# Second MLP up-projection: both halves of the activation in one 512-column pass, the convolution chain spread over later steps

## The reference

```python
def conv_ffn(h, w_up, conv_w, conv_b, w_down):
    S = h.shape[1]
    u = h @ w_up                                   # 2048 -> 2*5632
    up = jnp.pad(u, ((0, 0), (CONV_WIDTH - 1, 0), (0, 0)))
    y = conv_b
    for i in range(CONV_WIDTH):                    # 3 taps over the tokens
        y = y + up[:, i:i + S] * conv_w[i]
    a, g = jnp.split(y, 2, axis=-1)
    return (jax.nn.silu(g) * a) @ w_down           # 5632 -> 2048
# every layer:  x = x + g1 * mixer(modulate(rms_norm(x)));  x = x + g2 * conv_ffn(modulate(rms_norm(x)))
```

## Time and profile before

| | us |
|---|---|
| median of 3 runs | 2096.26 |
| lowest, highest | 2095.01, 2097.05 |
| profiled execution, first to last instruction | 2094.6 |
| PE busy in it | 2030.2 |
| DVE busy | 1631.6 |
| ACT busy | 1012.0 |

### The profile page before, as it was taken

One profiled execution on the slowest core, in us unless ns is written; L12 is line 12 of the kernel. 1 busy time (PEld: TensorE's weight loads), 2 busy tenths in 40 slices (PEclk: granted clock), 3 DMA queues, 4 the chain that ended last, 5 costly groups with the idle time before them and its releaser, 6 DMA issues.

```text
span 2094.6 us, 36723 instructions
## 1 busy us (share of the span) xinstructions
PE 2030.2 (97%) x13730; PEld 1876.4 (90%) x13730; DVE 1631.6 (78%) x2277; ACT 1012.0 (48%) x1347; POOL 308.1 (15%) x459
## 2 busy tenths in 40 slices
PE   3999999998999999999999999899999999999998
PEld 3888989888999889999899987799988999889986
DVE  5786898987899988898989977888765565556565
ACT  4323675545555444554445455554443454434453
POOL 3232342220111221121122100011000000000000
PEclk8999999999999999999999999999999999999999
DMA  9999899884889999888998874487655555565552
GB/s 360 355 356 329 299 336 331 298 308 173 303 313 317 333 349 338 297 308 310 363 326 322 314 268 140 141 298 279 239 190 188 185 185 184 182 200 165 197 181 101
DMA packets 235842, 558.28 MB, mean 267 GB/s; under 512 B 14024, under 2 KB 15032, under 8 KB 235192
## 3 DMA queue, kind: packets, MB, share of 16 engines
q1 hardware_dynamic: 180408, 355.03, 49.1%
q0 software_dynamic: 55296, 201.35, 26.7%
HBM read 554.23 MB, written 2.10 MB: 266 GB/s over the span
## 4 chain that ended last, share of the span: by engine, by line
PE 86%; DVE 6%; issue 3%; ACT 2%; DMA 2%; POOL 0%; DVEq 0%; ACTq 0%; POOLq 0%
PE ps L636 16%; PE ps L638 16%; PE ps L637 16%; PE ps L664 10%; PE ps L666 10%; PE ps L665 10%; PE ps L684 3%; DVE w_lo L1372 2%; DVE macc L1386 1%; PE ps L681 1%; PE ps L702 1%; DMA mraw<-in_w_mod 1%; ACT w_hi L1032 1%; ACT work L1032 1%; DMA early<-in_w_mod 1%
## 5 line engine op out<-in xcount | busy, mean ns | idle before, releaser
L1032 ACT ACTIVATE w_hi<-raw 128x1024 fp32r<-128x1024 f32 x640 | 666.1, 1056 | 769.3 <-PE ps L638 483.5
L1372 DVE TENSOR_TENSOR w_lo<-raw,w_hi 128x1024 fp32r<-128x1024 f32 x640 | 766.8, 1225 | 339.9 <-ACT w_hi L1032 339.3
L636 PE MATMUL ps<-h_hi,w_hi 128*128 128x256 f32 x3200 | 913.7, 286 | 1.4 <-DVE w_lo L1372 1.2
L638 PE MATMUL ps<-h_hi,w_lo 128*128 128x256 f32 x3200 | 906.7, 283 | 0.0
L637 PE MATMUL ps<-h_lo,w_hi 128*128 128x256 f32 x3200 | 906.7, 283 | 0.0
L636 PEld LDWEIGHTS ps<-h_hi,w_hi 128*128 128x128 f32 x3200 | 615.7, 192 | 4.9 <-issue 4.7
L637 PEld LDWEIGHTS ps<-h_lo,w_hi 128*128 128x128 f32 x3200 | 615.8, 192 | 2.1 <-issue 1.9
L638 PEld LDWEIGHTS ps<-h_hi,w_lo 128*128 128x128 f32 x3200 | 615.4, 192 | 0.0
L1386 DVE SCALAR_TENSOR_TENSOR macc<-mraw,cond,macc 128x512 f32<-128x512 f32 x620 | 427.8, 746 | 52.7 <-DMA mraw<-in_w_mod 44.4
L521 POOL DMA_DIRECT2D mraw<-in_w_mod x358 | 258.7, 723 | 1176.5 <-DVE macc L1386 868.4
L664 PE MATMUL ps<-w_hi,g_hi 128*128 128x512 f32 x832 | 326.1, 392 | 1.5 <-DVE w_lo L1372 1.5
(11 more groups left out here) (164 smaller groups left out, 1139.0 us busy)
## 6 DMA issues: line engine op xcount, KB each, us to landing
mraw<-in_w_mod POOLq DMA_DIRECT2D x358, 512.0 KB, 6.5
raw<-in_w_up SPq DMA_DIRECT2D x176, 1024.0 KB, 5.3
raw<-in_w_down SPq DMA_DIRECT2D x88, 1024.0 KB, 5.9
raw<-in_w_attn_in SPq DMA_DIRECT2D x48, 1024.0 KB, 8.7
raw<-in_w_attn_out SPq DMA_DIRECT2D x16, 1024.0 KB, 7.3
work<-in_w_mod POOLq DMA_DIRECT2D x12, 512.0 KB, 8.7
early<-in_w_mod POOLq DMA_DIRECT2D x8, 512.0 KB, 12.6
raw<-in_w_pool SPq DMA_DIRECT2D x4, 1024.0 KB, 5.4
```

The costliest lines, as they stand in the source:

```text
L636: mm(o, wh, ah, start=st, stop=False, skip_group_check=True)
L638: i = mm(o, wl, ah, start=False, stop=last_half and kk == 1, skip_group_check=True)
L1032: return nc.scalar.activation(o, i, f, **kw)
L1372: V.tensor_tensor(w_lo[:, s, :, :], raw[:, j % 4, h * 1024:(h + 1) * 1024].rearrange("p (k n) -> p k n", k=2), w_hi[:, s, :, :].bitcast(F3 ...
```

## The change

Layer 1's MLP becomes `mlp_second`, written out without hardware loops; layer 0's (`mlp_first`) stays as it was. In `mlp_second`:

- `h_hi` and `h_lo` become two halves of one tensor `h_pair`, and one matmul streams both (512 columns) against the same `w_hi`. Its result fills a whole bank: the first 256 columns hold high x high, the last 256 high x low. The third product (low x high, 256 columns) is added to the first 256.
- A half thus takes four banks: half 0 and half 1 of a pair have banks 0 to 3 and 4 to 7 or the reverse (`wide_bank`).
- ACT copies the last 256 columns of the four banks to `low` (SBUF), DVE adds the first 256 and frees the banks; the taps then read `low`.
- The taps are done a step later (`a` in step 4, `g` in step 0 of the next pair), silu and product in step 1, `g_hi` and `g_lo` in step 2; after the last pair of a block, in steps 0 to 2 of `down`.
- `gate_sum` comes before unit 3 of the next pair and writes bank 4; `gate_row` is in DVE's step 3; PE waits for it before half 1 (unit 4), which writes that bank.
- The last block's `down` takes its units in another order (`LAST_DOWN`).

```diff
-        h_hi = sb("h_hi", [P, KT, SEQ], F32R)
-        h_lo = sb("h_lo", [P, KT, SEQ], F32R)
+        h_pair = sb("h_pair", [P, KT, 2, SEQ], F32R)
+        h_hi, h_lo = h_pair[:, :, 0, :], h_pair[:, :, 1, :]
...
+        def wide_bank(block, half):
+            return (4 * (block % 2) + 4 * half) % 8
...
+        LAST_DOWN = [(0, 0), (0, 1), (1, 0), (1, 1), (0, 2), (1, 2),
+                     (2, 0), (2, 1), (2, 2), (3, 0), (3, 1), (3, 2)]
...
+            def unit_wide(q, j, k0, first, last, bank, h_need):
+                for half in range(2):
+                    pe.wait_ge(hlo_ready, h_need + k0 + 2 * half + 2)
+                    low_at, s0 = split_at(q, j)
+                    pe.wait_ge(lo_ready, low_at + half + 1)
+                    s = (s0 + half) % 4
+                    for kk in range(2):
+                        k = k0 + 2 * half + kk
+                        for t in range(4):
+                            wh, wl = (w[:, s, kk, t * P:(t + 1) * P] for w in (w_hi, w_lo))
+                            mm(ps[:, bank + t, :], wh, h_pair[:, k, :, :].rearrange("p a t -> p (a t)"),
+                               start=first and half == 0 and kk == 0, stop=False, skip_group_check=True)
+                            i = mm(ps[:, bank + t, 0:SEQ], wl, h_pair[:, k, 0, :], start=False,
+                                   stop=last and half == 1 and kk == 1, skip_group_check=True)
+                    i.then_inc(sub_used, 1)
...
+            def mlp_second():                      # PE
...
+                        for half in range(2):
+                            group_slot_free(g + 2 * i + half)
...
+                            if block == 0 and i and half:
+                                pe.wait_ge(mod_ready, 44 + i)
...
+                            for ks in range(4):
+                                if block == 0 and i and half == 0 and ks == 3:
+                                    group_slot_free(g + 2 * i + 1)
+                                    gate_sum(43 + i, i % 2)
+                                unit_wide(q + 2 * i + half, ks, 4 * ks, ks == 0, ks == 3,
+                                          wide_bank(block, half), KT * 3)
...
+                        for u in range(16):        # down, blocks 0 and 1
...
+                            pe.wait_ge(glo_ready, 2 * (11 + g0 + u % 4 + 1))
+                            unit_tok(q + u // 4, u % 4, 4 * (u % 4), u % 4 == 0, u % 4 == 3, g_hi, g_lo,
+                                     slot + u // 4 % 2)
...
+            def low_copy(used, bank, groups):      # ACT
+                act.wait_ge(sub_used, used)
+                if groups:
+                    act.wait_ge(taps_done, 2 * groups)
+                for b in range(2):
+                    A(low[:, 2 * b:2 * b + 2, :], ps[:, bank + 2 * b:bank + 2 * b + 2, SEQ:2 * SEQ],
+                      ACT.Copy).then_inc(low_out, 1)
...
+            def low_add(groups, bank):             # DVE
+                for b in range(2):
+                    dve.wait_ge(low_out, 2 * groups + b + 1)
+                    V.tensor_tensor(low[:, 2 * b:2 * b + 2, :], ps[:, bank + 2 * b:bank + 2 * b + 2, 0:SEQ],
+                                    low[:, 2 * b:2 * b + 2, :], ALU.add).then_inc((bank0_free, bank1_free)[b], 1)
...
+                    def pair_end(i, j):            # DVE
+                        if j == 0:
+                            earlier_taps(yg, 4 * p + FT, 8 * (11 + p) + 4, g + 2 * i + 1)
+                        elif j == 1:
+                            dve.wait_ge(taps_done, 4 * p + 2)
+                            gate_product(11 + p)
+                        elif j == 2:
+                            gated_lo(11 + p, i)
...
+                        for j in range(8):         # DVE, the steps of a pair
...
+                                piece(44 + i, at, (i + 1) % 2)
+                                piece(44 + i, at + 1, (i + 1) % 2)
+                            if not (p == 0 and j < 2):
+                                split(q + 2 * i, j + 2)
+                            if i and j < 3:
+                                pair_end(i - 1, j)
+                            if block == 0 and i and j == 3:
+                                gate_row(43 + i)
+                            if j == 4:
+                                earlier_taps(ya, 4 * p, 8 * (11 + p), g + 2 * i)
+                            if j % 4 == 3:
+                                low_add(2 * p + j // 4, wide_bank(block, j // 4))
```

More of the change, by code:

```diff
@@ L490, in _ @@
                     else:
[L491 to L495, removed]
+                        for u in range(12):
+                            cg, ks = LAST_DOWN[u] if l else divmod(u, 3)
+                            load(q + u // 4, u % 4,
+                                 w_down[l, 512 * (g0 + ks):512 * (g0 + ks) + 512, 512 * cg:512 * cg + 512])
                         q += 3
@@ L937, in mlp @@
                 for g0, n in BLOCKS:
-                    last_block = n == 3
-                    def up_pair(i):
-                        first = isinstance(i, int) and i == g0 == 0
+                    for i in range(n):
+                        first = i == g0 == 0
                         for half in range(2):
@@ L952, in up_pair @@
                                     transposes(nm, ks + 2)
-                        if l == 1 and g0 == 0:
-                            gate_sum(i + ch, 0)
-                    if l == 0 or g0 == 0:
-                        for i in range(n):
-                            up_pair(i)
-                    else:
-                        with pe.Fori(0, n) as i:
-                            up_pair(i)
                     q += 2 * n
                     g += 2 * n
-                    if not last_block:
+                    if n == 4:
                         for i in range(2):
@@ L1308, in up_pair @@
                         for b in range(2):
[L1309 to L1310 removed]
+                            act.wait_ge(gg_ready, 2 * (g0 + i) + b + 2)
+                            A(g_hi[:, 4 * i + 2 * b:4 * i + 2 * b + 2, :], yg[:, 2 * b:2 * b + 2, :],
                               ACT.Copy).then_inc(ghi_ready, 1)
[L1313 to L1320 removed]
                     q += 2 * n
@@ L1707, in up_pair @@
-                        if l == 1 and g0 == 0:
-                            gate_row(i + ch)
-                    if l == 0 or g0 == 0:
-                        for i in range(n):
-                            up_pair(i)
-                    else:
-                        with dve.Fori(0, n) as i:
-                            up_pair(i)
+                                    conv_taps(0, (ya, yg)[half], 4 * i + (4 * g0 + FT * half), half,
+                                              8 * (g0 + i) + 4 * half)
```

265 lines of the change are left out of this document (189 added, 76 removed).

## The result

The changed kernel takes 2109.93 us (median of 4 runs, 2107.55 to 2111.3) against 2096.4 us of the kernel before on the same chip: ratio 1.0069, interval 1.0058 to 1.0081. It is slower by about 14 us; 2096.2 was forecast, with a range up to 2104. The profiled execution has a span of 2108.0 us, against 2094.6.

A forecast was written before the change was run, and what follows sets the result against it. PE's matmul list and its new waits were taken to bound layer 1's MLP. Span: 2094.6 - 17.9 - 0.7 + 10.2 + 8.3 = 2094.5 us; the median lies 1.7 above, so 2096.2, range 2088 to 2104.

The forecast's parts named there:

- The two new waits: PE waits for `gate_row` before half 1, block 0 (three, +10.2 us) and for `g_lo` in down, blocks 0 and 1 (two, +8.3).
- Rival 2: One of the two kinds of new wait is absent: 2087.9 or 2086.0 us, with neither 2077.7; chance 0.18.
- rival 3: DVE falls behind in block 0, so splits come late for PE: 2100.2 to 2105 us; chance 0.06.
- the taps would take 0 to 0.1 us less out of SBUF: Convolution taps on DVE: 0 to 0.1 us less for each of 352, changing no wait.
- The hole after block 2: PE's 0.7 us wait after block 2's last pair goes: -0.7 us.
- each matmul costs its columns plus 0.0133 us, whatever its width: Up in layer 1's MLP: one matmul in three dropped, 1408 triples from 0.360 to 0.3467 us, 18.8 us less.
- the 17.9 us: Gain on PE's matmul list in up: 18.8 us less 0.9 lost in the first pair.
- Rival 4: In up, a wide matmul costs two narrow ones, 0.240 us, so the 17.9 us do not come: 2114.1; chance 0.02.
- My sum, with no fall of the clock or one: 0.62: Whole kernel: the summed terms hold, 2096.2 us, case between 2092 and 2100.4; chance 0.62.
- two falls or more: Rival: PE's clock drops to half rate in the new waits; two falls 2102.4 us, five 2111.7; chance 0.12.
- The price of 3.1 us a fall: Upper bound for one clock fall after a new PE wait: 6.9 us at 0.22 instead of 0.12 a matmul.
- The spread chain: Convolution chain in later steps, with ACT copies and 29 us of added DVE `low_add`: hidden, no cost beyond the new waits.

The follow-up runs named there:

- Experiments 1: Changed kernel with the gate's partition sum before unit 1 and `gate_row` at the head of DVE's step 2, ahead of its split: 2093.55 us, 0.9993 of the kernel before.
- experiment 2: Changed kernel with the last pair's `g_hi` and `g_lo` ahead of step 2's split in down of blocks 0 and 1: 2098.22 us, 1.0013 of the kernel before.
- experiment 6: Changed kernel with the moves of Experiments 1 and experiment 2 together: 2084.48 us, 0.9947 of the kernel before.
- experiment 7: experiment 6 with each wide pass replaced by two matmuls of 256 columns: 2095.36 us, 1.0003 of the kernel before.
- experiment 8: experiment 6 with the third pass also 512 columns wide, adding the low x low product: 2226.25 us in one run.
- experiment 3: Changed kernel with PE doing 13 or 15 unread 512-column matmuls ahead of each of the five waits: 2101.21 us, 1.0030 of the kernel before.
- experiment 5: Changed kernel with only the wide pass replaced by two matmuls of 256 columns: 2121.9 us, 1.0127 of the kernel before.
- experiment 11: experiment 6 with one unread fp32 matmul of 128 columns before each of the 14 groups of up in blocks 1 and 2: 2084.13 us, 0.9950 of the kernel before.
- experiment 4: experiment 3 with 6 and 7 filling matmuls instead of 13 and 15: 2103.07 us, 1.0036 of the kernel before.

## Why the prediction was wrong

**What bounds the kernel** held: PE's list, its waits and its clock account for the difference. DVE, ACT and DMA are not the limit outside the first pair and the two chains that the prediction named.

**The two new waits** held, place and mechanism: 17.5 us measured against 18.5, since the `g_lo` pair took 1.28 us and not 1.49, and `w_lo` started 1.08 us after ACT and not 1.18. Experiments 1 and 2 remove each by moving the one instruction and what feeds it. Rival 2 is out. So is rival 3: no other wait than the first pair's appeared, with DVE at 166 of 202 us in up 0, nor any of size in experiment 6, with 166 of 185. That the taps would take 0 to 0.1 us less out of SBUF changed nothing: they took 0.48 us against 0.47. The hole after block 2 went, as forecast.

**First failed step: "each matmul costs its columns plus 0.0133 us, whatever its width", and from it 3 x 0.120 becomes 0.3467.** The mechanism was right (experiment 7: the wide pass gains, experiment 8: 0.2267 for a wide one among its like), the size was off. In the changed kernel's alternation the couple costs 0.3533, half the gain of 0.0133 a triple, in all of blocks 1 and 2. Of the 17.9 us, 11.4 arrived between experiments 7 and 6, where block 0 runs mostly at the quick pitch, and about 9 in the changed kernel. By stretch it lacks 3.4 in up 1, 2.6 in up 2 and about 2.9 in up 0 (the 6.8 of the table less three falls of 1.56, plus 0.3 of shorter waits and the 0.5 of the `gate_sum` that moved to down 0): 8.9 us. As a check, 20 groups of 64 couples at 0.0067 more are 8.5. Rival 4 named this place but with the whole gain lost; the truth was half. What failed in the argument is that two uniform streams were read as the price of a mixed one, and rows for a mixed one did not exist, so both ends belonged in the range around the sum. Why the alternation has two rates stays open.

**Second failed step: "My sum, with no fall of the clock or one: 0.62", against 0.12 for two falls or more.** The sum puts the clock at nothing; all five waits had a fall. The bounds had been read correctly (full clock after 1.9 us, half after 5.1), but 3.4 and 4.2 lie between them, and nothing in the rows favoured the upper side so strongly. "PE is full up to its start and from its end" was taken as evidence against, and was none: experiment 3 shows that with the wait filled the falls are gone. That all five had one was partly chance: of the 15 waits of this length in the changed kernel and experiments 1, 2 and 5, 13 had a fall. The price of 3.1 us a fall was given as a bound, and holds as one: a fall of 3.4 us costs 1.56 (3.4 x (1 - 0.12 / 0.22) is 1.5), one of 6.8 us 2.9. The changed kernel's five lasted 3.4 us each: 7.8 us.

**The sum again**, from the forecast span of 2094.5: + 8.9 (pitch) + 7.8 (clock) - 1.0 (waits) - 2.4 (the untouched stretch ahead) = 2107.8, against 2108.0. Either error alone would have left the time near the upper end of the range; it took both to leave it.

**The spread chain** as such was costed at nothing, and experiment 7 agrees within 2 us: 1.0003. What the change loses is the place in the order of two instructions, `gate_row` and the last pair's `g_lo`: with both moved it is 0.9947 of before, with both moved and eight of a width in a row it is 0.9924.

## What to carry to other kernels

When work moves later on a list that has waits for PE in it, look for instructions that stood ahead of such a wait and now stand behind it: if PE's next unit needs one of them, the whole hand-over chain (here 3.3 and 3.8 us) opens each time, and its cure is a place one step up, not a faster instruction. Price a new PE idle time of over 3 us together with the clock that may follow it (here 1.6 us, at worst 2.9), and, where the wait can't be removed, give PE matmuls whose result nobody reads. A matmul's price taken from a stream of equal ones was the lower bound for the mixed stream here, not its price.

## What the runs showed of the hardware

- The same alternation of 512 and 256 columns, each with its own weights, runs at 0.3467 or at 0.3533 us a couple, at a granted clock of 1.00 both times. The slow rate held for whole blocks, and single groups changed it where the stream was interrupted (experiment 11). Streams of one width have one rate: 0.120 and 0.2267.
- In the changed kernel the granted clock fell not in the idle time but 0.2 to 1.4 us after PE was back at work, to 0.5 for 3.4 us. In experiments 1 and 5 five of six falls began 0.4 to 0.8 us before the restart, and three of the six lasted 6.8 us. Behind idle times of 3.3 and 3.8 us it fell in 5 of 5 cases with the change and in 5 of 5 in experiment 5, but in 2 of 3 in experiment 2 and in 1 of 2 in experiment 1; behind 1.6 to 2.0 us in 1 of 5 (experiment 4). So the length of the idle time alone does not decide.
- A fall of 3.4 us costs about 1.6 us, somewhat under half of what the idle time itself costs here; one of 6.8 us cost 2.9.
